# Output and down projections of a decoder layer with tokens on the partitions, and the second norm by rows

## What is computed

```python
x  = x + gate1 * (merged @ w_out)                    # merged (512, 1024), w_out (1024, 1024)
h2 = rms_norm(x, norm2_g) * (1 + scale2) + shift2
up = h2 @ w_up                                       # w_up (1024, 5632)
y  = causal depthwise conv of width 3 over the tokens, on up
x  = x + gate2 * ((silu(a) * b) @ w_down)            # a, b = halves of y; w_down (2816, 1024)
```

## Time and profile before

| | us |
|---|---|
| median of 3 runs | 777.43 (777.32 to 779.0) |
| the profiled execution, its own time | 777.76 |
| its span, first to last instruction | 776.0 |
| TensorE matmuls busy | 748.4, 96% of the span |
| VectorE busy | 377.7, 49% |
| GpSimd busy | 358.1, 46% |
| ScalarE busy | 308.2, 40% |

### The profile page before, as it was taken

How to read it: one execution, slowest core, us unless ns; L and a number is a source line. 1 busy time by engine, 2 the same in 40 slices (tenths; PEclk the granted TensorE clock), 3 DMA queues, 4 the chain that set the end, 5 groups by cost and what they waited for, 6 DMA issues and landing times.

```text
span 776.0 us, 9536 instructions
## 1 busy us (share of the span) xinstructions
PE 748.4 (96%) x3618; PEld 604.4 (78%) x3618; DVE 377.7 (49%) x682; ACT 308.2 (40%) x496; POOL 358.1 (46%) x187
## 2 busy tenths in 40 slices
PE   4889999999989999999999999999999999999998
PEld 2367788787777778888877888888888888888886
DVE  2562499954657872558937444545343433000000
ACT  4234423437655753333236344443344343222121
POOL 1125368346556583544943443444343444444250
PEclk9979999999999999999999999999999999999999
DMA  8933113231043343545755332233233321232401
GB/s 327 368 110 110 55 54 97 68 108 41 15 163 109 109 148 124 168 158 180 229 177 175 109 109 83 80 109 109 76 87 109 108 95 64 87 108 95 124 27 55
DMA packets 94461, 91.72 MB, mean 118 GB/s; under 512 B 2003, under 2 KB 85711, under 8 KB 94415
## 3 DMA queue, kind: packets, MB, share of 16 engines
q1 hardware_dynamic: 92239, 82.71, 33.5%
q10 hardware_dynamic: 2176, 8.39, 3.2%
HBM read 89.00 MB, written 2.10 MB: 117 GB/s over the span
## 4 chain that ended last, share of the span: by engine, by line
PE 76%; DVE 11%; issue 3%; DMA 3%; POOL 2%; ACT 2%; SPq 2%; ACTq 0%; DVEq 0%; POOLq 0%
PE bank L1374 45%; PE bank L1383 22%; DVE work L1158 2%; PE bank L1405 2%; DVE top L1155 2%; DMA ada<-in_w_ada_dram 2%; DVE macc L1047 2%; PE bank L1464 1%; PE bank L1410 1%; DVE prob L1265 1%; POOL wsplit L589 1%; PE bank L1629 1%; SPq L514 1%; DMA ada_mid<-in_w_ada_dram 1%; PE bank L1608 1%
## 5 line engine op out<-in xcount | busy, mean ns | idle before, releaser
L589 POOL TENSOR_TENSOR wsplit<-stage,wsplit 128x1024 fp32r<-128x1024 f32 (+2 forms) x127 | 288.8, 2279 | 370.9 <-ACT wsplit L700 370.9
L1374 PE MATMUL bank<-hT,wsplit 128*128 128x512 f32 x1200 | 286.9, 391 | 0.0
L1374 PEld LDWEIGHTS bank<-hT,wsplit 128*128 128x128 f32 x1200 | 223.9, 188 | 46.2
L700 ACT ACTIVATE wsplit<-stage 128x1024 fp32r<-128x1024 f32 (+2 forms) x127 | 125.5, 991 | 305.4 <-PE bank L1383 292.2
L1383 PE MATMUL bank<-hT,wsplit 128*128 128x512 f32 x600 | 150.0, 392 | 0.0
L1383 PEld LDWEIGHTS bank<-hT,wsplit 128*128 128x128 f32 x600 | 111.5, 188 | 23.8 <-issue 0.6
L1374 PE MATMUL bank<-guT,wsplit 128*128 128x512 f32 x352 | 84.0, 390 | 0.0
L1374 PEld LDWEIGHTS bank<-guT,wsplit 128*128 128x128 f32 x352 | 65.9, 188 | 13.5
L1336 DVE SCALAR_TENSOR_TENSOR yb<-bank,conv,yb 128x511 f32<-128x511 f32 (+1 forms) x44 | 33.0, 749 | 65.7 <-ACT yb L969 64.8
L1336 DVE SCALAR_TENSOR_TENSOR ya<-bank,conv,ya 128x511 f32<-128x511 f32 (+1 forms) x44 | 33.0, 750 | 60.4 <-ACT ya L969 59.7
L1361 DVE SCALAR_TENSOR_TENSOR xT<-bank,mod,xT 128x512 f32<-128x512 f32 x8 | 6.0, 751 | 111.5 <-PE bank L1383 111.5
(11 more groups left out here) (182 smaller groups left out, 812.3 us busy)
## 6 DMA issues: line engine op xcount, KB each, us to landing
stage<-in_w_up_dram SPq DMA_DIRECT2D x44, 512.0 KB, 5.0
stage<-in_w_in_dram SPq DMA_DIRECT2D x17, 1024.0 KB, 5.1
ada_mid<-in_w_ada_dram ACTq DMA_DIRECT2D x8, 1024.0 KB, 5.8
stage<-in_w_down_dram SPq DMA_DIRECT2D x8, 1024.0 KB, 5.2
ada<-in_w_ada_dram SPq DMA_DIRECT2D x7, 1024.0 KB, 11.7
stage<-in_w_ada_dram SPq DMA_DIRECT2D x4, 1024.0 KB, 5.2
stage<-in_w_out_dram SPq DMA_DIRECT2D x4, 1024.0 KB, 7.1
ada_last<-in_w_ada_dram SPq DMA_DIRECT2D x4, 1024.0 KB, 8.5
```

The lines of the kernel that those rows point to most:

```text
L589: pool.tensor_tensor(unit_split(n, 1), unit_source(n), unit_split(n, 0).bitcast(F32), ALU.subtract).then_inc(low, 1)
L700: me.did(act.activation(unit_split(n, 0), unit_source(n), ACT.Copy), high)
L1374: pe.matmul(out_bank[:, :], hi[:, k, :], rhs[:, part, k0 + k, :], start=first and k == 0 and part == 0, stop=False)
```

## The change

Both projections turn around: a 128-token block of the activations (128 input features by 128 tokens) is the stationary operand, and 512 output columns of the weight are moved past it. A result is a PSUM bank of 128 tokens by 512 features, so there are 4 token tiles times 2 halves of the features for each projection. A unit of weights is now 2 blocks of input features by 512 columns, of the same size as before.

- `x` stays by rows in `xtok`; the residual of a tile is a multiplication from PSUM by the gate, as a row that all partitions hold (`gate_row`), and an addition into `xtok`. The gate rows come from a load that repeats the bias on all partitions, and from two matmuls with a matrix of ones (`gate_sums`), in place of `mod_columns(2)` and `mod_columns(5)`.
- `w_out`, first half of the features: four tiles side by side in banks 3 to 6, unit by unit. Second half: its four units lie in places of their own (`own`), and the tiles come one after another. After a tile its row is scaled by the inverse root (ACT), transposed by TensorE in eight blocks (`x2_turn`), given gain and shift (`h2_full`, DVE), and split in high (ACT) and low (DVE) parts.
- The first three products of `w_up` run on 256 tokens at a time.
- `mod_rows(3, 3)` and all four `mod_rows(4, q)` stand ahead of the first residual in DVE's program; `scale2` is accumulated in a buffer of its own. `mod_columns(3)` and `mod_columns(4)` stand inside the first and second tile of the second half, the latter behind a wait for `mod_ok` 3, which `mod_vector(3)` gives.
- `w_down` likewise: four tiles side by side for each half of the features, stored by rows. `out_turn`, `store_copy`, `keep_clock`, `token_squares`, the second `spread_roots` and POOL's sums of squares are gone.

```diff
@@ schedule
-    for m in range(KD):
-        s.product("wo", m)
+    for half in range(2):
+        for k0 in range(0, KD, 4):
+            s.block_rows("out", k0, k0 + 4, half, (lambda n: ("own", n)) if half else None)
...
@@ gpsimd
-            for m in range(1, KD - 1):
...
-                pool.tensor_tensor(sqsum[:, :], sqsum[:, :], sq2[:, m % 2, :], ALU.add).then_inc(x2_add, 1)
             low_parts(len(sch.units))
@@ scalar
             load_mid(0)
+            act.dma_start(gate_row[:, :], b_ada[0:1, 2 * D:3 * D].to_broadcast([P, D])).then_inc(gate_in, 16)
             load_mid(1)
...
+            for n, upto in enumerate((sch.unit["out", 0, NT - 1], sch.unit["out", 1, 0], sch.unit["out", 1, 1],
+                                      sch.unit["out", 1, NT - 1])):
+                load_mid(n + 4)
+                high_parts(upto + 1)
...
+            me.did(act.activation(tstat[:, 2, 0:1], ones[:, 0:1], ACT.Sqrt))
+            for t in range(NT):
+                square_half(0, t)
+            high_parts(sch.unit["ua", 1])
+            for t in range(NT):
+                square_half(1, t)
+                token_root(t)
+                scaled(t)
+                if t == 0:
+                    high_parts(sch.unit["ua", 1] + 1)
+                if t:
+                    h2_high(t - 1)
+            h2_high(NT - 1)
@@ vector
-            mod_vector(2)
+            gate_vector(0)
...
+            def residual(n, half, t, done, waits, into, signal):
+                cols = slice(half * S, (half + 1) * S)
+                dve.wait_ge(done, waits)
+                me.did(dve.tensor_tensor(into[0], banks[sch.bank[sch.chunk[n, half, t]]][:, :], gate_row[:, cols],
+                                         ALU.mult), drained["dve"])
+                me.settle()
+                me.did(dve.tensor_tensor(into[1], into[0], xtok[:, t, cols], ALU.add), signal)
...
+            mod_rows(3, 3)
+            for q in range(KD // 2):
+                mod_rows(4, q)
+            for t in range(NT):
+                wo_residual(0, t)
...
+            for t in range(NT):
+                wo_residual(1, t)
+                if t:
+                    if t == 1:
+                        mod_vector(4)
+                        dve.wait_ge(gain_ok, 2)
+                    h2_full(t - 1)
+                token_inverse(t)
+                if t == 0:
+                    mod_vector(3)
+                if t:
+                    h2_low(t - 1)
+            h2_full(NT - 1)
+            h2_low(NT - 1)
@@ tensor
+            def tile_products(n, out_bank, rows_of, t, k0, first, last):
+                pe.wait_ge(high, n + 1)
+                pe.wait_ge(low, n + 1)
+                for r in range(sch.units[n][0]):
+                    for a, b in THREE:
+                        mm = pe.matmul(out_bank[:, :], rows_of[:, a, k0 + r, t * P:(t + 1) * P],
+                                       unit_split(n, b)[:, r, :], ...)
...
             def mod_columns(j):
                 pe.wait_ge(mod_sum, KD * j)
...
+                if j == 4:
+                    pe.wait_ge(mod_ok, 3)
...
+            for t in range(NT):
+                name = ("wo", 1, t)
                 await_bank(pe, name)
+                for pair in range(NT):
+                    mm = tile_products(sch.unit["out", 1, pair], bank(name), merged, t, 2 * pair, pair == 0,
+                                       pair == NT - 1)
...
+                    if t < 2 and pair == 1:
+                        mod_columns(3 + t)
+                if t:
+                    x2_turn(t - 1)
+
+            firsts = (("ua", 0), ("ub", 0), ("ua", 1))
+            for half in range(2):
+                pe.wait_ge(h2_lo, NT * (half + 1))
+                for n, name in enumerate(firsts):
...
+                    high_products(sch.unit[name], bank(name), hT, HALVES[half])
+                    low_products(sch.unit[name], bank(name), hT, HALVES[half], (None, used)[half])
+                    if half == 0 and n == 1:
+                        x2_turn(NT - 1)
```

More of the change, by code:

```diff
@@ L109, in __init__ @@
         self.bank = []
+        self.ring = -1
+        self.home = []
+        self.ringed = 0
         self.before = []
@@ L131, in split, with block_rows, opens @@
             self.unit[name] = len(self.units) - 1
-    def opens(self, name, drain):
-        n = len(self.chunk)
[L136 to L139, removed]
+    def block_rows(self, w, k0, k1, half, home=None):
+        item = self.stage(w, (half * S,), k0, k1, NT)
+        for part in range((k1 - k0) // 2):
+            self.units.append((2, part, S))
+            self.house(home and home(k0 // 2 + part))
+            self.item_of.append(item)
+            self.last_use[item] = ("unit", len(self.units))
+            self.unit[w, half, k0 // 2 + part] = len(self.units) - 1
+    def opens(self, name, drain, at=None):
+        n = len(self.chunk)
+        if at is None:
+            banks = NBANK - 1 if name in FILLERS else NBANK
+            at = self.ring = (self.ring + 1) % banks
+        self.before.append(max((k for k in range(n) if self.bank[k] == at), default=None))
+        self.bank.append(at)
         self.chunk[name] = n
@@ L184, in schedule @@
             s.opens((kind, m), "dve")
[L185 to L192, removed]
+    for half in range(2):
+        for k0 in range(0, KF, 4):
+            s.block_rows("down", k0, min(k0 + 4, KF), half)
+        for t in range(NT):
+            s.opens(("dn", half, t), "dve", (3 + t, None)[half] if not half or t < NT - 1 else 7)
     return s
@@ L463, in unit_source @@
         def unit_source(n):
-            nk, part = sch.units[n]
+            nk, part, columns = sch.units[n]
             item = sch.item_of[n]
@@ new lines, in wo_residual @@
+            def wo_residual(half, t):
+                cols = slice(half * S, (half + 1) * S)
+                if t == NT - 1:
+                    done, waits = used, sch.unit["out", half, NT - 1] + 1
+                else:
+                    done, waits = wo_done, half * (NT - 1) + t + 1
+                residual("wo", half, t, done, waits, (tmp[:, t % 2, :], xtok[:, t, cols]), x2_ok)
+            mod_rows(3, 3)
+            for q in range(KD // 2):
+                mod_rows(4, q)
+            for t in range(NT):
+                wo_residual(0, t)
@@ L1433, in spread_roots @@
                 mm.then_inc(root_b, 1)
-            def keep_clock(n, weights, moving):
-                for _ in range(n):
-                    pe.matmul(PT[1][:, :], weights, moving, start=True, stop=True)
             def row_products(q, rows_q, out_banks):
```

430 lines of the change are left out of this document (237 added, 193 removed).

## The result

| | before | after |
|---|---|---|
| median, us | 777.58 (4 runs, 777.32 to 779.0) | 787.47 (4 runs, 786.28 to 788.03) |
| profiled execution: own time / span, us | 777.76 / 776.0 | 788.03 / 786.0 |
| stretch, first `wo` matmul to the end of the third `w_up` product | 347.8 to 423.8: 76.0 | 348.27 to 437.28: 89.0 |
| from there to the last matmul | 347.3 | 344.67 |
| last matmul to the end | 4.93 | 4.05 |

The ratio is 1.0121, with a 95% interval of 1.0104 to 1.0139: slower by 1.2%, 0.6 us above the forecast.

A forecast was written before the change was run, and what follows sets the result against it. TensorE, busy 96% of the span, was taken to bound the kernel. The stretch's +12.4 and -2.9 elsewhere made +9.5: span 785.5, execution 787.3, median 786.9 us, range 778 to 792.

The forecast's parts named there:

- The forecast case: TensorE waits at mod_columns(4) and the clock falls: chance 0.65, its own range 784 to 791 us.
- Where the wait ends: At mod_columns(4): DVE finishes rows at 384.6, five residuals at 392.2, and gives mod_ok 3 at 395.1.
- TensorE's arrival: In the second half of w_out: TensorE stands at mod_columns(4) at 386.2 and waits 8.9 us.
- 2.1 + 2.3 + 2.3 us: In tile 0 of w_out's second half: TensorE's waits for the low parts of units 5, 6 and 7.
- the rival of 802: In the first w_up products: 256 columns cost as much time as 512, 15.4 us more; chance 0.03.
- 38.1 + 3.0: From mod_ok 3 at 395.1 to the third w_up product's end at 433.2, plus 3.0 us for the clock: 436.2.
- 1.7 for `h2_full`: In DVE's work per tile: eight instructions on 128 columns, at 0.87 us for four, take 1.7 us.
- 1.3 and 0.7: In the DVE and ACT ping-pong: DVE comes out 1.3 us behind, and 0.7 before the second 256 tokens.
- 3.0 us lost: Behind the wait at mod_columns(4): 6 us of half clock lose 3.0 us; bounds none and 18 us of half speed.
- The rule on transposes: Transposes don't count as clock activity; the eight before tile 2 would add about 1 us, giving 788; left out of the sum.
- The repeated gate row: At gate 1: lands 7.5 us after issue, costing nothing up to 10; rival of a later landing, 788 to 795, chance 0.05.
- The overlap works: At mod_columns(4): mod_ok 3 comes early enough, rows done by 378; 775, or 766 with no wait; chance 0.1.

The follow-up runs named there:

- experiment 1: Changed kernel with mod_columns(4) writing to bank 3, so it no longer waits for mod_vector(3): 783.14 us, ratio 1.0076.
- the third order: Changed kernel, columns in bank 3, ACT and DVE lists reordered, mod_columns(4) inside tile 2, rows (4,2) and (4,3) before wo_residual(1, 1): 772.29 us, ratio 0.9923.
- the reordered kernels: Four versions of the changed kernel with columns in bank 3 and the same work in other orders: 775.37, 776.55, 772.29 and 775.91 us.
- all four orders: The four reorderings of the changed kernel's same work, all with mod_columns(4) writing to bank 3: ratios from 0.9923 to 0.9994.
- experiment 4: Changed kernel with DVE doing the four first-half residuals and mod_vector(3) ahead of rows (4,2) and (4,3): 784.96 us, ratio 1.0099.
- experiment 2: Changed kernel with matmuls whose result nobody reads ahead of mod_columns(4): 785.5 us with 40, 787.86 us with 28.

## Why the prediction was right

The forecast case came: a wait at `mod_columns(4)` that DVE's `mod_vector(3)` ends, and half clock behind it. Point by point:

- **Where the wait ends.** Forecast 395.1, measured 392.5. The rows ended 2.1 us early (382.5 for 384.6; the loads landed in 5.5, median), and a residual took 1.33 for 1.5. ACT stood between as forecast: the square of tile 0's second half waits behind two high parts.
- **TensorE's arrival.** Forecast 386.2, measured 383.2. The step that failed is "2.1 + 2.3 + 2.3 us" for the low parts: the waits were 1.64 and 0.88. I put one low part of 2.4 us behind each load; measured, the last two high parts came together and POOL ran three in a row (9.0 us). Both ends came some 3 us early, so the wait was 9.5 for 8.9, a result better than its terms.
- **TensorE's own pieces.** 96 matmuls in 21.77 (21.8). A product on 256 tokens takes 2.88 us, 0.120 each: exact, and the rival of 802 fell with it.
- **From the wait's end to the stretch's end.** Forecast 38.1 + 3.0, measured 44.6 (392.69 to 437.28). Here two terms were mis-sized. "1.7 for `h2_full`": it took 2.65, since the rows it was sized by (eight times 0.22 for 128 columns from SBUF) read SBUF, and these read PSUM (0.33 each). With it a tile's round on DVE is 8.1 and 7.7 us (400.64, 408.75, 416.44), 2.3 of them waits for ACT (0.36 and 1.92), where TensorE's is 6.3, and the waits are 0.93 + 1.19 and 0.83 instead of 1.3 and 0.7. And "3.0 us lost" to the clock: the columns took 3.41 for 1.70, the 12 matmuls 4.34 for 2.72, and the first 16 on 256 tokens, behind the waits of the exchange, 3.42 for 1.92: 4.8 us in all. I had forecast one fall, and there were two (0.50 from 386 to 399, 0.59 and 0.56 from 416 to 420). The waits account for 0.95 of the 3.5 us over the forecast and the clock for 1.8; the other 0.7 is spread over the two tiles (5.56 and 5.70 for 5.4) and the products.
- **The total.** That it came out within 0.6 us is partly luck: the wait ended 2.6 us earlier than forecast, counted from the start of the span, and what follows it took 3.5 us longer.
- **The rule on transposes** that the prediction weighed (the Trainium skill, TensorE: Matmul & The Clock Gate, "Part 4: PE-mode transpose") had nothing to act on: the clock was back before the first eight transposes at 400.44 and stayed at 1.00 through them. In experiment 1 eight transposes did stand in a low stretch (392.49, right behind a wait of 5.36 us), and the clock was back at about 398, 5.3 us after they began; in the kernel after it was back 6.6 us after the one-column matmuls began. That doesn't bear the rule out, and one execution of each doesn't refute it.
- **Elsewhere.** Three pairs of transposes less: -2.6, as forecast. The tail is 4.05 for 4.6, because the last residuals, 1.36 apart, ended 1.5 after the last matmul, not 2.0. The repeated gate row landed in 7.0 us (7.5): DVE was idle for it for 8.3 us, until 310.9, but TensorE ran on. That the down projection is worth these 3.5 us is read from the traces; it wasn't tried alone.
- **The rivals.** "The overlap works" was held to need rows done by 378. That step is wrong as to what is possible: the third order has the rows done at 392.8 and still ends the stretch 12 us sooner, since there `mod_columns(4)` stands in tile 2, writes to bank 3 and no longer waits for `mod_vector(3)`. The rival was right only for the order as written. Its 775 is about what the reordered kernels gave.

So the order theory holds: the same work, with the columns in another bank, gave 787.5 and 772.3. The exchange theory has a part: the round of DVE and ACT leaves a wait of 0.8 us before the second 256 tokens in all four orders, and without the split it costs 10 us more. What stays open: how much of the loss would go if DVE and POOL never met (not tried), what the move to bank 3 is worth inside the new orders, and why the clock falls in some executions of a kernel and not in others.

## What to carry to other kernels

When a change moves work between engines, the busy shares say little: list, for the stretch, what each engine's program puts ahead of the signal that the bound engine waits for, and ask of each item whether the signal needs it. A result that needs only an early input (here the columns of `macc_scale`) should not share a bank, and so a semaphore, with one that comes late. Dummy matmuls never give back the wait itself, and what they do for the clock depends on where they end: here 40 that reached past the end of the wait kept it, and 28 that ended 3.15 us ahead of it gained nothing.

## What the runs showed of the hardware

- DVE and POOL hinder each other in both directions where both of DVE's inputs lie in SBUF. An addition of 128x512 took 0.69 us alone and 2.15 beside a low part (experiment 4), a row of 1024 up to 3.28 for 1.29 and one element for each partition 0.85 for 0.15 (both in the kernel after), and the `gs` row of 8 columns 2.34 for 0.17 (experiment 1, 394.04). POOL's low part took 2.35 alone and about 3.0 in a row of three or four beside DVE (9.01 for three, 11.86 for four). The multiplications from PSUM stayed at 0.67 to 0.69 throughout. I had expected this for the rows, not for a single element.
- A clock that has held through an idle gap can still fall just after it: 1.00 through 3.15 us of idle, 0.50 from 392 on, when TensorE had been at work again for 1.4 us (experiment 2, the run with 28 matmuls).
